# Splitting 1024-column weight tiles in one piece instead of two halves, in a two-layer transformer kernel on one Trainium2 core

## The chip, the cores and the metric

The kernel runs on one core of one Trainium2 chip. The metric is device time in microseconds for one call; smaller is better. The engines named here are PE (TensorE, matrix products; PEld is its weight load), ACT (ScalarE), DVE (VectorE), POOL (GpSimd) and SP (SyncE, which issues most DMAs). They run side by side, each through its own list of instructions in order, and meet at semaphores.

## What is computed

A trunk of two layers on 256 tokens of width 1024, in float32. Each layer has attention and then a product-key expert retrieval (PEER) over 16384 experts. The kernel does not gather the chosen experts; it multiplies by the whole tables and uses gates that are zero for the experts not chosen.

```python
q = xt @ w_q                                   # 8 heads, 2 x 128 wide
sc = q . sub_keys                              # 128 scores per head and side
v1,i1 = top_k(sc[:,:,0],16); v2,i2 = top_k(sc[:,:,1],16)
top_v, top_pos = top_k(all sums v1+v2, 16)     # expert index eidx = i1*128+i2
gates = softmax(top_v)
a = gelu(u_tab[eidx] @ x) * gates              # u_tab, v_tab: (16384, 1024)
out = sum_k a * v_tab[eidx]
```

## The kernel before

Each layer ends with `experts(l)`, and that part is most of the time. It has two passes, each over 128 tiles (`NKEY`) of 128 x 1024 float32, 512 KB each: the up pass (products with u, then GELU, spilled to DRAM as `s_store`), and the down pass (the spilled values come back, are weighted by the gates, and are multiplied with v). For accuracy each weight tile is split into `hi` (the value rounded to fp32r) and `lo` (the rest), and each product is made of three: hi with hi, hi with lo, lo with hi.

How one tile n travels:

- SP loads it into `raw`, a ring of four (`load_u`, `load_v`, lines 289 and 292), once the tile four before it has been lowered. In the up pass each load is followed by `spill` (L296), which stores the GELU result of eight tiles earlier. In the down pass each load follows a `fetch` (L302) of a spilled tile.
- ACT copies `raw` to `hi` (`split`, L742). `hi` and `lo` are rings of two, so tile n can be split only once PE has used tile n-2; this is counted by `w_used`. Before, a tile is two halves of 512 columns, each with its own split and its own wait on `w_used`.
- DVE writes `lo = raw - hi` (`lower`, L1061), again in two halves.
- PE runs `up` (24 matmuls of 256 columns, 12 per half) or `down` (12 matmuls of 512 columns, 6 per half). It waits for `hi_done` and `lo_done` ahead of each half, and raises `w_used` after each half.

What else stands in the queues, in program order:

- ACT in the up pass, step n: split half 0 of tile n+2, `gelu(n)` (L748; it waits for the spill of tile n-4 to land), split half 1 of tile n+2. In the down pass, step j: `split_a(j+1)` (L770, the hi part of the activations), then both halves of tile j+2.
- DVE in the down pass, step j: `weigh(j+2)` (L1075), `lower_a(j+1)` (L1080), then `lower` of tile j+2. In layer 0 every fourth step adds `next_modulation` (L1085 and L1088), a row of the next layer's modulation. PE's `down(j)` waits for `a_hi`, `a_lo`, `hi` and `lo` of tile j, in this order.
- DVE in the first 38 up tiles: the retrieval (top-16 searches, then `choose`). The heads 0 to 4 are done before; those of heads 5 to 7 (48 pieces) and `choose` (21 pieces) are a generator with an estimated cost per piece, 500 to 1200 ns. After each lowered half `advance(700)` takes pieces until their estimates reach 700; an overshoot is not carried over. `choose` has eight comparisons (L1045), each followed by a product on POOL (L400). It needs `q_e` from ACT (an Exp, L794), which stands between two loops of up steps.
- After tile 37 PE does `picks`; tiles 40 to 103 each have a group of matmuls, a `one_hot` on DVE and a `copy_gates` on ACT (L764); tiles 104 to 127 are plain up steps.

Of the kernel before, what the change touches and what calls it, by code (L numbers as in the profile page):

```python
# [15 lines left out]
P = 128  # L16
# [92 lines left out]
def build(nc, a, out):  # L109

    with ExitStack() as ctx:
# [155 lines left out]
        def _(sp):  # L267
# [19 lines left out]
            for l in range(LAYERS):  # L287
# [32 lines left out]
                for n in range(4, 8):  # L320
                    sp.wait_ge(s[l]["lo_done"], 2 * n - 6)
# [9 lines left out]
                for n in range(NKEY, NKEY + 8):  # L331
                    if n >= NKEY + 5:
                        fetch(n - NKEY - 1, (n - 1) % 4, 1)
                    sp.wait_ge(s[l]["lo_done"], 2 * n - 6)
# [3 lines left out]
                def down_loads(j, i, r):  # L338
                    fetch(j - 1, (r - 1) % 4, i - (1 if r == 0 else 0))
                    sp.wait_ge(s[l]["lo_done"], STREAM - 6 + 2 * j)  # L340
# [16 lines left out]
                sp.wait_ge(s[l]["lo_done"], 2 * STREAM)  # L357
# [46 lines left out]
        def _(pe):  # L404
# [148 lines left out]
            def experts(l):  # L553

                def up(n, r, wait=True):
# [23 lines left out]
                def down(j, r, first=False, end=False):  # L579

                    pe.wait_ge(s[l]["ah_done"], j + 1)
                    pe.wait_ge(s[l]["al_done"], j + 1)
                    for h in range(2):
                        pe.wait_ge(s[l]["hi_done"], STREAM + 2 * j + h + 1)
                        pe.wait_ge(s[l]["lo_done"], STREAM + 2 * j + h + 1)
# [6 lines left out]
                        last.then_inc(s[l]["w_used"], 1)  # L592
# [57 lines left out]
        def _(act):  # L650
# [67 lines left out]
            for l in range(LAYERS):  # L718
# [47 lines left out]
                def split_a(j, r, b, wait=True):  # L766
                    act.wait_ge(s[l]["a_ready"], j + 1)
                    if wait:
                        act.wait_ge(s[l]["w_used"], STREAM + 2 * j - 2)
# [6 lines left out]
                for h in range(PH):  # L776
# [8 lines left out]
                    if h in (4, 5):  # L785
                        for half in range(2):
                            split(h - 4, h - 4, half, 0, False)
# [19 lines left out]
                def down_step(j, r, round_, wait=True, more=True):  # L807
                    split_a(j + 1, r + 1, (r + 1) % 4, wait)
                    if more:
                        nr, nround = (r + 2) % 4, round_ + (r + 2) // 4 + NKEY // 4  # L810
                        for h in range(2):
                            split(NKEY + 2 + j, nr, h, nround)
# [8 lines left out]
                for n in range(0, 4, 2):  # L821
                    act.wait_ge(s[l]["w_used"], 2 * STREAM)
# [5 lines left out]
        def _(dve):  # L828
# [227 lines left out]
            def experts(l):  # L1056

                def lower(n, r, h):
                    dve.wait_ge(s[l]["hi_done"], 2 * n + h + 1)
                    c = slice(h * HALF, (h + 1) * HALF)  # L1060
                    v.tensor_tensor(lo[:, r % 2, c], raw[:, r, c], hi[:, r % 2, c].bitcast(F32), ALU.subtract).then_inc(s[l]["lo_done"], 1)  # L1061
# [39 lines left out]
                for h in range(PLAIN_HEADS):  # L1101
                    for _ in retrieve_head(l, h):
                        pass
                    if h == 3:
                        for n in range(2):
                            for half in range(2):
                                lower(n, n, half)
                for n in range(GROUP_AT - 2):
                    for half in range(2):
# [207 lines left out]
```

## Time and profile before

| what | value |
|---|---|
| median of 3 runs | 2355.55 us (2352.31 to 2356.49) |
| the profiled execution | 2345.75 us, its span 2343.8 us |
| PE busy | 2114.5 us (90%) |
| DVE busy | 1505.0 us (64%) |
| ACT busy | 1026.7 us (44%) |
| matmuls of the down pass, a_hi with hi | 1024 of 396 ns |
| lowered halves, splits | 1024 of 690 ns, 1024 of 629 ns |

Times in the trace are microseconds from the start of the span. A row of a timeline has: start, duration, engine, line, operation, output<-inputs, shape, count, and in brackets the idle time of the engine ahead of it and what ended it. Matmuls overlap in the engine, so the distance from one start to the next is the time that one costs; the end of a matmul is modelled.

### The profile page before, as it was taken

The numbers are of one execution on the slowest core, as the hardware profiler recorded it, in microseconds if no ns is written. First come the engines' busy times: TensorE is split into PE (matmuls) and PEld (weight loads), VectorE is DVE, ScalarE is ACT, GpSimd is POOL, SyncE is SP. The second block draws the span as 40 slices with busy tenths as digits, with TensorE's granted clock in tenths as the row PEclk, the third lists the DMA queues.
The fourth block names the chain that finished last, engine by engine and source line by source line (L and its number), as shares of the span: only waits on it lengthen the run. The fifth ranks groups of instructions, "written<-read, shape, count | busy, mean of one in ns | idle before, by whom it ended". The sixth has DMA issues, their size and how long they took to land.

```text
span 2343.8 us, 43649 instructions
## 1 busy us (share of the span) xinstructions
PE 2114.5 (90%) x12524; PEld 1860.3 (79%) x12524; DVE 1505.0 (64%) x3632; ACT 1026.7 (44%) x2019; POOL 62.9 (3%) x55
## 2 busy tenths in 40 slices
PE   1997699799999988888898889979999999999997
PEld 0844589799999976767676667979999998888886
DVE  5433778627777457777775226883677755777776
ACT  1013124535555445455453222345455554555554
POOL 0000000300000000000000000030000000000000
PEclk7976799899999999999999989989999999999999
DMA  7851426446555678788772213445455567777774
GB/s 262 337 214 72 135 90 190 145 123 174 173 175 172 205 243 287 275 296 295 284 255 77 90 72 108 144 144 170 135 171 176 172 197 231 238 240 237 239 240 150
DMA packets 168450, 447.24 MB, mean 191 GB/s; under 512 B 18624, under 2 KB 85440, under 8 KB 163792
## 3 DMA queue, kind: packets, MB, share of 16 engines
q1 hardware_dynamic: 163472, 393.17, 52.8%
q0 software_dynamic: 4928, 53.45, 5.7%
q8 instruction: 26, 0.43, 0.1%
q14 instruction: 24, 0.20, 0.0%
HBM read 409.84 MB, written 36.70 MB: 191 GB/s over the span
## 4 chain that ended last, share of the span: by engine, by line
PE 73%; DVE 12%; DMA 7%; ACT 4%; issue 3%; SPq 1%; ACTq 0%; DVEq 0%
PE bank L406 72%; DMA s_store<-work 3%; DVE lo L1061 3%; DMA wmod_ring<-s_store 2%; DVE big L1045 2%; ACT hi L742 2%; DMA wmod_ring<-in_w_mod 1%; DVE wmod_ring L1085 1%; ACT big L697 1%; ACT a_hi L770 1%; DVE wmod_ring L1075 1%; PE bank L461 1%; DVE big L906 0%; DVE work L848 0%; DVE big L997 0%
## 5 line engine op out<-in xcount | busy, mean ns | idle before, releaser
L1061 DVE TENSOR_TENSOR lo<-raw,hi 128x512 fp32r<-128x512 f32 x1024 | 697.3, 690 | 460.8 <-ACT hi L742 455.8
L742 ACT ACTIVATE hi<-raw 128x512 fp32r<-128x512 f32 x1024 | 634.7, 629 | 507.9 <-PE bank L406 505.5
L406 PE MATMUL bank<-x_hi,hi 128*128 128x256 f32 x2048 | 599.9, 293 | 39.6 <-DVE lo L1061 25.7
L406 PE MATMUL bank<-x_lo,hi 128*128 128x256 f32 x2048 | 582.5, 284 | 0.0
L406 PE MATMUL bank<-x_hi,lo 128*128 128x256 f32 x2048 | 582.0, 284 | 0.0
L406 PE MATMUL bank<-hi,a_hi 128*128 128x512 f32 x1024 | 405.1, 396 | 52.5 <-ACT a_hi L770 48.9
L406 PEld LDWEIGHTS bank<-x_hi,hi 128*128 128x128 f32 x2048 | 394.4, 193 | 52.3 <-issue 45.1
L406 PE MATMUL bank<-hi,a_lo 128*128 128x512 f32 x1024 | 402.1, 393 | 0.0
L406 PE MATMUL bank<-lo,a_hi 128*128 128x512 f32 x1024 | 401.5, 392 | 0.0
L406 PEld LDWEIGHTS bank<-x_lo,hi 128*128 128x128 f32 x2048 | 395.4, 193 | 0.2
L406 PEld LDWEIGHTS bank<-x_hi,lo 128*128 128x128 f32 x2048 | 394.9, 193 | 0.0
L406 PE MATMUL bank<-raw,big 128*128 128x256 f32 (+1 forms) x1248 | 285.0, 389 | 68.2 <-ACT raw L673 53.5
L406 PEld LDWEIGHTS bank<-raw,big 128*128 128x128 f32 (+1 forms) x1248 | 241.4, 195 | 107.2 <-issue 55.8
L406 PEld LDWEIGHTS bank<-hi,a_hi 128*128 128x128 f32 x1024 | 193.0, 188 | 115.0 <-ACT hi L742 54.5
L748 ACT ACTIVATE work<-bank 128x256 f32<-128x256 f32 x256 | 98.4, 384 | 308.1 <-DMA s_store<-work 190.7
L406 PEld LDWEIGHTS bank<-hi,a_lo 128*128 128x128 f32 x1024 | 193.3, 189 | 42.3
L406 PEld LDWEIGHTS bank<-lo,a_hi 128*128 128x128 f32 x1024 | 193.5, 189 | 35.5
L1069 DVE TENSOR_SCALAR wmod_ring<-cst,wmod_ring 128x128 f32<-128x128 f32 x512 | 142.2, 341 | 0.0
L406 PE MATMUL bank<-wmod_ring 128*128 128x128 f32 x1024 | 135.1, 275 | 0.0
L406 PEld LDWEIGHTS bank<-wmod_ring 128*128 128x128 f32 x1024 | 125.7, 192 | 0.0
L1075 DVE TENSOR_TENSOR wmod_ring<-wmod_ring,big 128x256 f32<-128x256 f32 x256 | 107.2, 419 | 13.5 <-DMA wmod_ring<-s_store 13.3
L1080 DVE TENSOR_TENSOR a_lo<-wmod_ring,a_hi 128x256 fp32r<-128x256 f32 x256 | 106.9, 417 | 0.0
(138 smaller groups left out, 1432.4 us busy)
## 6 DMA issues: line engine op xcount, KB each, us to landing
raw<-in_u SPq DMA_DIRECT2D x256, 512.0 KB, 3.8
raw<-in_v SPq DMA_DIRECT2D x256, 512.0 KB, 3.9
wmod_ring<-in_w_mod SPq DMA_DIRECT2D x96, 512.0 KB, 4.6
s_store<-work SPq DMA_DIRECT2D x256, 128.0 KB, 3.6
wmod_ring<-s_store SPq DMA_DIRECT2D x256, 128.0 KB, 3.5
big<-in_w_in POOLq DMA_DIRECT2D x10, 2048.0 KB, 11.1
big<-in_w_q POOLq DMA_DIRECT2D x16, 1024.0 KB, 6.2
big<-in_w_out POOLq DMA_DIRECT2D x2, 4096.0 KB, 12.8
```

The costliest lines, as they stand in the source:

```text
L406: return nc.tensor.matmul(o, w, x, start=start, stop=stop, skip_group_check=free)
L461: last = nc.tensor.transpose(bank[4 + n % 2][:, c * P:(c + 1) * P], scores[:, i, c * P:(c + 1) * P], ident)
L697: last = f(c, c, ACT.Exp, bias=neg[:, 2 * i + t:2 * i + t + 1], accum_out=den[:, 2 * i + t:2 * i + t + 1])
L742: f(hi[:, r % 2, c], raw[:, r, c], ACT.Copy).then_inc(s[l]["hi_done"], 1)
L748: f(work[:, r, :], bank[4 + r % 2][:, 0:T], ACT.Gelu).then_inc(s[l]["s_gelu"], 1)
L770: f(a_hi[:, r % 2, :], back[:, b, :], ACT.Copy).then_inc(s[l]["ah_done"], 1)
L1045: v.tensor_tensor(q_hot[n // 2].rearrange("p h k a -> p (h k) a")[:, c], q_abf[side][:, t, c].unsqueeze(2).to_broadcast([P, 64, TOPK]), io ...
L1061: v.tensor_tensor(lo[:, r % 2, c], raw[:, r, c], hi[:, r % 2, c].bitcast(F32), ALU.subtract).then_inc(s[l]["lo_done"], 1)
L1069: ins = v.tensor_scalar(hot[r % 2][:, 1, n, :], iota, pick[:, 1, bass.ds(4 * g + n, 1)], pick[:, 2, bass.ds(4 * g + n, 1)], ALU.is_equal, ...
L1075: v.tensor_tensor(back[:, b, :], back[:, b, :], gates[:, bass.ds(j, 1), :].rearrange("p a t -> p (a t)"), ALU.mult)\
L1080: v.tensor_tensor(a_lo[:, r % 2, :], back[:, b, :], a_hi[:, r % 2, :].bitcast(F32), ALU.subtract).then_inc(s[l]["al_done"], 1)
L1085: v.tensor_tensor_reduce(wmod_ring[:, r, :], wmod_ring[:, r, :], c_all[:], 1.0, 0.0, ALU.mult, ALU.add, tile_sum[:, r:r + 1]).then_inc(s[1 ...
```

## The change

Every weight tile is split and lowered whole: one `split` (ACT) and one `lower` (DVE) of 1024 columns, one pair of waits and one increment of `w_used` per tile on PE. All thresholds on `hi_done`, `lo_done` and `w_used` are counted in tiles. In an up step ACT does `split(n+2)` and then `gelu(n)`. `advance(700)` after each half becomes `advance(1400)` after each tile, and the Exp of the gates moves from behind up step 15 to behind up step 23. The diff is cut to its core; the other hunks change thresholds and loops in the same way.

```diff
@@ -318,11 +318,11 @@
                 with sp.Fori(2, NKEY // 4) as i:
                     for r in range(4):
-                        sp.wait_ge(s[l]["lo_done"], 8 * i + 2 * r - 6)
+                        sp.wait_ge(s[l]["lo_done"], 4 * i + r - 3)
                         load_u(4 * i + r, r)
                         spill(4 * i + r - 8, r)
                 sp.wait_ge(s[l]["hot_used"], GROUPS)
...
@@ -557,15 +557,14 @@
                     o = bank[4 + r][:, 0:T]
-                    for h in range(2):
-                        pe.wait_ge(s[l]["hi_done"], 2 * n + h + 1)
-                        pe.wait_ge(s[l]["lo_done"], 2 * n + h + 1)
-                        for k in range(h * KT // 2, (h + 1) * KT // 2):
-                            c = slice(k * P, (k + 1) * P)
-                            mm(o, hi[:, r, c], x_hi[:, k, :], k == 0, False)
-                            mm(o, hi[:, r, c], x_lo[:, k, :], False, False)
-                            last = mm(o, lo[:, r, c], x_hi[:, k, :], False, k == KT - 1)
-                        last.then_inc(s[l]["w_used"], 1)
+                    pe.wait_ge(s[l]["hi_done"], n + 1)
+                    pe.wait_ge(s[l]["lo_done"], n + 1)
+                    for k in range(KT):
+                        c = slice(k * P, (k + 1) * P)
+                        mm(o, hi[:, r, c], x_hi[:, k, :], k == 0, False)
+                        mm(o, hi[:, r, c], x_lo[:, k, :], False, False)
+                        last = mm(o, lo[:, r, c], x_hi[:, k, :], False, k == KT - 1)
+                    last.then_inc(s[l]["w_used"], 1)
...
@@ -580,16 +579,16 @@
                     pe.wait_ge(s[l]["al_done"], j + 1)
+                    pe.wait_ge(s[l]["hi_done"], NKEY + j + 1)
+                    pe.wait_ge(s[l]["lo_done"], NKEY + j + 1)
                     for h in range(2):
-                        pe.wait_ge(s[l]["hi_done"], STREAM + 2 * j + h + 1)
-                        pe.wait_ge(s[l]["lo_done"], STREAM + 2 * j + h + 1)
                         c = slice(h * HALF, (h + 1) * HALF)
                         for t in range(TT):
                             o, tok = bank[2 * t + h][:, :], slice(t * P, (t + 1) * P)
                             mm(o, a_hi[:, r, tok], hi[:, r, c], first, False, True)
                             mm(o, a_hi[:, r, tok], lo[:, r, c], False, False, True)
                             last = mm(o, a_lo[:, r, tok], hi[:, r, c], False, end, True)
-                        last.then_inc(s[l]["w_used"], 1)
+                    last.then_inc(s[l]["w_used"], 1)
...
@@ -734,24 +733,22 @@
-                def split(n, r, h, round_, wait=True):
+                def split(n, r, round_, wait=True):
                     act.wait_ge(raw_in[r], 16 * (round_ + 1) + 16 * l * (STREAM // RAWS))
                     if wait:
-                        act.wait_ge(s[l]["w_used"], 2 * n + h - 3)
-                    c = slice(h * HALF, (h + 1) * HALF)
-                    f(hi[:, r % 2, c], raw[:, r, c], ACT.Copy).then_inc(s[l]["hi_done"], 1)
+                        act.wait_ge(s[l]["w_used"], n - 1)
+                    f(hi[:, r % 2, :], raw[:, r, :], ACT.Copy).then_inc(s[l]["hi_done"], 1)
 
                 def gelu(n, r, round_, wait=True):
-                    act.wait_ge(s[l]["w_used"], 2 * n + 2)
+                    act.wait_ge(s[l]["w_used"], n + 1)
                     if wait:
                         act.wait_ge(s_out[r], 16 * round_ + 16 * l * (NKEY // STAGES))
                     f(work[:, r, :], bank[4 + r % 2][:, 0:T], ACT.Gelu).then_inc(s[l]["s_gelu"], 1)
 
                 def up_step(n, r, round_, wait=True):
                     nr, nround = (r + 2) % 4, round_ + (r + 2) // 4
-                    split(n + 2, nr, 0, nround)
+                    split(n + 2, nr, nround)
                     gelu(n, r, round_, wait)
-                    split(n + 2, nr, 1, nround)
 
...
@@ -783,16 +780,15 @@
-                up_steps(4, 16)
+                up_steps(4, 24)
                 act.wait_ge(s[l]["gate_max"], 1)
                 f(q_e[:], q_e[:], ACT.Exp).then_inc(s[l]["gate_exp"], 1)
-                up_steps(16, GROUP_AT)
+                up_steps(24, GROUP_AT)
...
@@ -1055,10 +1050,9 @@
-                def lower(n, r, h):
-                    dve.wait_ge(s[l]["hi_done"], 2 * n + h + 1)
-                    c = slice(h * HALF, (h + 1) * HALF)
-                    v.tensor_tensor(lo[:, r % 2, c], raw[:, r, c], hi[:, r % 2, c].bitcast(F32), ALU.subtract).then_inc(s[l]["lo_done"], 1)
+                def lower(n, r):
+                    dve.wait_ge(s[l]["hi_done"], n + 1)
+                    v.tensor_tensor(lo[:, r % 2, :], raw[:, r, :], hi[:, r % 2, :].bitcast(F32), ALU.subtract).then_inc(s[l]["lo_done"], 1)
...
@@ -1103,12 +1097,10 @@
                 for n in range(GROUP_AT - 2):
-                    for half in range(2):
-                        lower(n + 2, (n + 2) % 4, half)
-                        advance(700)
+                    lower(n + 2, (n + 2) % 4)
+                    advance(1400)
...
                 def down_step(j, r, round_, mods=None, weighs=True, lowers=True):
                     if weighs:
                         weigh(j + 2, (r + 2) % 4, round_ + (r + 2) // 4)
                     lower_a(j + 1, r + 1, (r + 1) % 4)
                     if lowers:
-                        for half in range(2):
-                            lower(NKEY + 2 + j, (r + 2) % 4, half)
+                        lower(NKEY + 2 + j, (r + 2) % 4)
```

## Rows read from the trace of the kernel before

**Rows 1.** The chain that ended last, shares of the span by engine.

```profile
PE 73%; DVE 12%; DMA 7%; ACT 4%; issue 3%; SPq 1%; ACTq 0%; DVEq 0%
```

**Rows 2.** Stages: start:end, length, busy of PE, PEld, DVE, ACT, POOL; clock, DMA, GB/s.

```profile
356.57:439.36 82.79, 67.89 (x495) 63.72 (x494) 78.29 (x213) 36.87 (x68) 22.06 (x8) 0.92 0.54 164
771.00:844.50 73.50, 70.51 (x577) 69.51 (x576) 32.19 (x51) 34.80 (x73) 0.00 (x0) 1.00 0.72 214
844.50:1256.40 411.90, 362.67 (x1536) 286.67 (x1536) 298.95 (x606) 202.54 (x382) 3.76 (x7) 0.99 0.77 272
1971.40:2325.00 353.60, 353.27 (x1536) 288.47 (x1536) 260.49 (x508) 199.56 (x382) 0.00 (x0) 1.00 0.73 234
```

**Rows 3.** Groups by line and shape: count, busy us, mean ns, idle before.

```profile
L1208 DVE TENSOR_TENSOR x_lo<-raw,x_hi 128x2048 fp32r<-128x2048 f32 x2 | 4.6, 2294 | 5.1 <-ACT x_hi L735 5.1
L735 ACT ACTIVATE x_hi<-raw 128x2048 fp32r<-128x2048 f32 x2 | 3.8, 1910 | 0.1
```

**Rows 4.** Timeline of the down pass, layer 1, at the end of a tile.

```profile
2102.18 0.40 PE L406 MATMUL bank<-hi,a_hi 128*128 128x512 f32 x1
...
2102.38 0.63 ACT L742 ACTIVATE hi<-raw 128x512 fp32r<-128x512 f32 x1 [0.75 <-PE bank L406]
2102.41 0.40 PE L406 MATMUL bank<-lo,a_hi 128*128 128x512 f32 x1
...
2103.05 0.69 DVE L1061 TENSOR_TENSOR lo<-raw,hi 128x512 fp32r<-128x512 f32 x1 [0.69 <-ACT hi L742]
...
2103.66 0.42 DVE L1075 TENSOR_TENSOR wmod_ring<-wmod_ring,big 128x256 f32<-128x256 f32 x1
...
2103.99 0.42 DVE L1080 TENSOR_TENSOR a_lo<-wmod_ring,a_hi 128x256 fp32r<-128x256 f32 x1
```

**Rows 5.** Timeline of the down pass, layer 0, from one modulation step to the next.

```profile
1015.02 0.47 PE L406 MATMUL bank<-hi,a_hi 128*128 128x512 f32 x1 [1.23 <-ACT a_hi L770]
...
1018.06 0.63 ACT L742 ACTIVATE hi<-raw 128x512 fp32r<-128x512 f32 x1 [0.75 <-PE bank L406]
...
1023.51 0.63 ACT L742 ACTIVATE hi<-raw 128x512 fp32r<-128x512 f32 x1 [0.73 <-PE bank L406]
...
1024.78 1.22 DVE L1085 CUSTOM_DVE_ANT_0 wmod_ring<-wmod_ring,c_all 128x1024 f32<-128x1024 f32 x1
...
1026.65 0.42 DVE L1080 TENSOR_TENSOR a_lo<-wmod_ring,a_hi 128x256 fp32r<-128x256 f32 x1
...
1027.42 0.47 PE L406 MATMUL bank<-hi,a_hi 128*128 128x512 f32 x1 [1.21 <-ACT a_hi L770]
```

**Rows 6.** Timeline of DVE, POOL and PE in the first up tiles, layer 0.

```profile
359.23 0.69 DVE L1061 TENSOR_TENSOR lo<-raw,hi 128x512 fp32r<-128x512 f32 x1 [5.02 <-ACT hi L742]
...
400.23 0.42 DVE L1019 TENSOR_TENSOR big<-big 128x256 f32<-128x256 f32 x1
...
438.54 2.48 DVE L1061 TENSOR_TENSOR lo<-raw,hi 128x512 fp32r<-128x512 f32 x4
...
408.13 2.75 POOL L400 TENSOR_TENSOR big<-big 128x1024 f32<-128x1024 f32 x1 [83.47 <-DVE big L1045]
...
408.56 3.40 DVE L1045 TENSOR_TENSOR big<-big,cst 128x1024 f32<-128x1024 f32 x1
...
411.89 0.68 DVE L1061 TENSOR_TENSOR lo<-raw,hi 128x512 fp32r<-128x512 f32 x1
...
412.71 0.43 PE L406 MATMUL bank<-x_hi,hi 128*128 128x256 f32 x1 [2.26 <-DVE lo L1061]
```

**Rows 7.** Timeline of ACT and PE where a loop of up steps begins anew, layer 0.

```profile
466.62 1.28 ACT L742 ACT_TABLE_LOAD   x1
...
470.48 0.36 PE L406 MATMUL bank<-x_hi,hi 128*128 128x256 f32 x1 [1.05 <-ACT work L748]
```

**Rows 8.** Timeline of DVE and ACT in the last up tiles, layer 0.

```profile
820.60 1.29 DVE L1061 TENSOR_TENSOR lo<-raw,hi 128x512 fp32r<-128x512 f32 x2 [1.83 <-ACT hi L742]
...
825.70 0.38 ACT L748 ACTIVATE work<-bank 128x256 f32<-128x256 f32 x1 [1.75 <-DMA s_store<-work]
```

More of the change, by code:

```diff
@@ L320, in _ @@
                 for n in range(4, 8):
-                    sp.wait_ge(s[l]["lo_done"], 2 * n - 6)
+                    sp.wait_ge(s[l]["lo_done"], n - 3)
                     load_u(n, n % 4)
@@ L333, in _ @@
                         fetch(n - NKEY - 1, (n - 1) % 4, 1)
-                    sp.wait_ge(s[l]["lo_done"], 2 * n - 6)
+                    sp.wait_ge(s[l]["lo_done"], n - 3)
                     load_v(n - NKEY, n % 4)
@@ L339, in down_loads @@
                     fetch(j - 1, (r - 1) % 4, i - (1 if r == 0 else 0))
-                    sp.wait_ge(s[l]["lo_done"], STREAM - 6 + 2 * j)
+                    sp.wait_ge(s[l]["lo_done"], NKEY - 3 + j)
                     load_v(j, r)
@@ L356, in _ @@
                 fetch(NKEY - 1, 3, NKEY // 4 - 1)
-                sp.wait_ge(s[l]["lo_done"], 2 * STREAM)
+                sp.wait_ge(s[l]["lo_done"], STREAM)
                 sp.dma_start(raw[:, 0:2].rearrange("p a n -> p (a n)"), x_store).then_inc(x_back, 16)
@@ L768, in split_a @@
                     if wait:
-                        act.wait_ge(s[l]["w_used"], STREAM + 2 * j - 2)
+                        act.wait_ge(s[l]["w_used"], NKEY + j - 1)
                     f(a_hi[:, r % 2, :], back[:, b, :], ACT.Copy).then_inc(s[l]["ah_done"], 1)
@@ L785, in _ @@
                     if h in (4, 5):
-                        for half in range(2):
-                            split(h - 4, h - 4, half, 0, False)
+                        split(h - 4, h - 4, 0, False)
                 copy_keys(PH - 1)
@@ L810, in down_step @@
                         nr, nround = (r + 2) % 4, round_ + (r + 2) // 4 + NKEY // 4
-                        for h in range(2):
-                            split(NKEY + 2 + j, nr, h, nround)
+                        split(NKEY + 2 + j, nr, nround)
                 for r in range(4):
@@ L821, in _ @@
                 for n in range(0, 4, 2):
-                    act.wait_ge(s[l]["w_used"], 2 * STREAM)
+                    act.wait_ge(s[l]["w_used"], STREAM)
                     f(yt[:, n // 2, 0:512], bank[n][:, :], ACT.Copy).then_inc(s[l]["e_copied"], 1)
@@ L1105, in experts @@
                         for n in range(2):
-                            for half in range(2):
-                                lower(n, n, half)
+                            lower(n, n)
                 for n in range(GROUP_AT - 2):
-                    for half in range(2):
-                        lower(n + 2, (n + 2) % 4, half)
-                        advance(700)
+                    lower(n + 2, (n + 2) % 4)
+                    advance(1400)
                 for _ in left:
@@ L1118, in experts @@
                 for g in range(4):
-                    for half in range(2):
-                        lower(GROUP_AT + g, g, half)
+                    lower(GROUP_AT + g, g)
                     one_hot(g, g, g >= 2)
@@ L1123, in experts @@
                     for r in range(4):
-                        for half in range(2):
-                            lower(GROUP_AT + 4 * i + r, r, half)
+                        lower(GROUP_AT + 4 * i + r, r)
                         one_hot(4 * i + r, r)
@@ L1128, in experts @@
                     for r in range(4):
-                        for half in range(2):
-                            lower(4 * i + r, r, half)
+                        lower(4 * i + r, r)
                 dve.wait_ge(s[l]["g_copied"], GROUPS)
@@ L1135, in experts @@
                         lower_a(0, 0, 0)
-                    for half in range(2):
-                        lower(NKEY + n, n, half)
+                    lower(NKEY + n, n)
                 def down_step(j, r, round_, mods=None, weighs=True, lowers=True):
@@ L1143, in down_step @@
                     if lowers:
-                        for half in range(2):
-                            lower(NKEY + 2 + j, (r + 2) % 4, half)
+                        lower(NKEY + 2 + j, (r + 2) % 4)
                     if mods:
@@ L1213, in _ @@
                 for n in range(1, 4, 2):
-                    dve.wait_ge(s[l]["w_used"], 2 * STREAM)
+                    dve.wait_ge(s[l]["w_used"], STREAM)
                     v.tensor_copy(yt[:, n // 2, 512:1024], bank[n][:, :]).then_inc(s[l]["e_copied"], 1)
```

## The prediction, made before the changed kernel was run

> **What bounds the kernel now.** I read the chain that ended last first: PE has 73% of it [rows 1], so what counts is whether PE waits. The second view is the table of stages [rows 2]. In the down pass of layer 1 PE is busy 353.27 of 353.60 us: 128 tiles at 2.76 us, PE alone is the bound. In the down pass of layer 0 it is busy 362.67 of 411.90 us, in the last 24 up tiles 70.51 of 73.50, and in the first 20 or so up tiles 67.89 of 82.79. The third view is the timeline of one tile in each of these, to see how late hi and lo come. A tile n can only be split when tile n-2 has been used. So each tile closes a loop with the one two before it: S(j+2) = S(j) + one tile of PE + the chain ACT, DVE, PE. PE hides this chain as long as the loop is shorter than two PE tiles. That is what the change touches.
>
> **The down pass, the loop before.** Sizes, start to start: split of the last half to its lower 0.67 (2102.38 to 2103.05), lower to weigh 0.61 (to 2103.66), weigh to lower_a 0.33 [rows 4]; lower_a itself 0.42, and from its end to PE's first matmul 0.35 (1026.65 + 0.42 = 1027.07, to 1027.42) [rows 5]. Together 2.38. From a tile's first matmul to the split that its end releases: 1018.06 - 1015.02 = 3.04 where PE had stood still before it [rows 5]; the 12 matmuls step by 0.23, so that is 2.76 + 0.08 for the start from rest + 0.20 of hand-over; without rest 2.95. Loop: 2.95 + 2.38 = 5.33, against 2 x 2.76 = 5.52. PE hides it with 0.19 to spare, as layer 1 shows. The same sum tells the modulation step of layer 0: 1023.51 to 1027.42 = 3.91, which is 2.38 + 1.53 for L1085 and L1088, and four tiles take 1027.42 - 1015.02 = 12.40, not 11.04 [rows 5].
>
> **The loop after.** The last half is no longer all that is left when a tile ends; the whole tile is. A split of 1024 columns: 630 ns at 512 [rows 4] and 1910 at 2048 [rows 3] give 0.834 ns a column and 1056 ns, 0.43 more than a half. A lower: 690 at 512 (0.69 in the rows) [rows 4] and 2294 at 2048 [rows 3] give 1.04 ns a column and 1225 ns, 0.535 more. The loop grows by 0.96 to 6.29 us, and PE, which now rests once a loop, adds its 0.08: 6.37 for two tiles, 3.19 a tile (one of the two tiles waits, the other starts right behind it). Layer 1: 128 x (3.19 - 2.76) = +55 us. Layer 0, four tiles: the loop with the modulation is 6.37 + 1.53 = 7.90, the other 6.37, together 14.27 against 12.40; 32 times 1.87 = +60 us. Layer 0 also has waits that are not of this loop: 411.90 - 32 x 12.40 = 15 us, mostly late fetches beside POOL's large loads. A fetch is asked for three tiles ahead, which are now 1.4 us longer; I let half of it (8 us, bounds 0 and 15) disappear: +52. The two waits and one increment fewer on PE cost nothing now: across the middle of two tiles' halves the matmuls step by 0.23 (2102.18 to 2102.41) as everywhere [rows 4], so nothing is gained.
>
> The Trainium skill, TensorE: Matmul & The Clock Gate, "The cost: per-tile semaphore tail", says that increments of packed matmuls serialize at some 26 ns each. For 512 increments fewer that would be an estimate of 13 us gained; the rows above show no such step here.
>
> **The up pass, plain tiles.** The 24 matmuls step by 0.12: 2.88 a tile. The loop is 2.88 + 0.20 + 1.10 (split to lower) + 1.225 + 0.14 (lower's end to PE: 411.89 + 0.68 is 412.57, PE starts at 412.71 [rows 6]) = 5.55, below 5.76: hidden by 0.2. `gelu` now stands behind the split. That removes a stall: before, the second half's split stood behind `gelu`, and `gelu` behind the spill's landing (lowered 821.3, gelu 825.70 [rows 8]), a loop of about 6.0 for two tiles. After, gelu(n) is due at S(n) + 4.1 and must be done by S(n) + 5.8, and the next split is due only then. The last 24 tiles go from 73.5 us [rows 2] to 24 x 2.88 = 69.1 and a little at the change of pass: -4 a layer. The 64 group tiles take 3.76 each (group and up), so the loop has nearly 2 us to spare: nothing.
>
> **The first 40 up tiles.** Here DVE sets the pace: the pieces of the retrieval stand between the lowers. Before, 359.23 to 400.23 for 12 tiles (4 pieces a tile: the estimates are 500 and 550, so two pass each 700) is 3.4 us a tile; then `choose` to 438.54 [rows 6], with 12 halves of 0.60 in it, so 31.1 us of its own. There each L1045 takes 3.32 instead of 1.2 because a POOL product (2.75) runs first [rows 6]. After, three pieces a tile: 1.66 (41.0 less 24 x 0.60, over 48 pieces, x 3) + 1.145 = 2.81, below PE's 2.88. The 48 pieces last 16 tiles at PE's pace, and `choose` takes 7 tiles: 31.1 + 7 x 1.145 = 39.1. Reckoned from tile 0 at 356.57 [rows 2]: lower(18) at 356.57 + 16 x 2.88 + 4.2 = 406.8, lower(25) at 445.9, PE in tile 25 at 447.3, thirteen tiles later `picks` at 484.7. Before, PE was in the middle of tile 20 at 439.36, 17.5 tiles ahead of `picks` (489.8), and lost 1.05 on three restarts of the ACT loop, where two table loads of 1.28 stand ahead of the split and the gelu [rows 7], and some more beside them; by its matmuls `picks` began at about 495.8. After, the first of these loads runs ahead of the wait and the second behind the split; bank and ring bear 0.2. Gain 11; I take 9, because PE now rests 4.8 us at a stretch in `choose`, and the clock, 0.92 in this stage [rows 2], may be longer at its lower level; -9 a layer, bounds 0 and -16 (two L1045 side by side might leave POOL out). The Exp moved behind step 23 is early enough: step 23 ends some 3.5 us before lower(24), and `choose` asks for it after that. No queue is moved otherwise; SP's loads and spills wait for the same tiles, lowered at most 0.5 us later, with over 5 us to spare.
>
> The Trainium skill, VectorE: DVE Perf Modes, "The TRN2 errata", says that an instruction with its source in SBUF pays a fixed latency, and that larger tiles spread it; that speaks for the change. The rows agree: two lowered halves take 1.29 [rows 8], a whole one 1.225. It pays only where DVE is the bound.
>
> **Sum.** +55 + 52 - 2 x 4 - 2 x 9 = +81. On the profiled execution (span 2343.8, 2345.75 us in all) that is 2427; the median of the runs shown is 2355.55, 0.4% above that execution, and a difference carries over: 2355.55 + 81 = 2437.
>
> **Rivals.** (A) The loop stays hidden. It decides at a chain of 2 x 2.76 - 2.95 = 2.57 from split to PE; I have 3.34. If weigh and lower_a (0.75) turned out not to lie on it, for instance because DVE does them while the whole split runs, the down pass costs nothing and the gains remain: 2355.55 - 26 = 2330, faster. Against: in program order they stand behind `lower` of the tile, and the 12.40 of layer 0 comes out only with them. Chance 0.04. (B) A shorter loop: the 0.20 of hand-over and the 0.08 are not paid by a warm pipeline: 0.14 less a tile, 256 tiles, 36 us less: 2401. Against: 3.04 is measured. Chance 0.12. (C) The gains don't come (9 a layer lost to the slower clock and to POOL in the way of the longer lowers) and the 8 us of late fetches stay: 2355.55 + 81 + 26 = 2463. Chance 0.14. (D) The middle of a tile costs PE something after all: at most 0.01 a boundary by [rows 4], 512 boundaries, 5 us: 2432. Chance 0.02.
>
> **Chances and range.** The forecast has 0.68, its own range being +-14 by the bounds above. The range from B to nearly C, 2403 to 2460, leaves out A and part of B and C, some 0.2. A measurement of this kernel tells about 0.2% (5 us) from no change; faster 0.04 (A), within 0.01, slower 0.95.
>
> **What would show it.** In layer 1's down pass: one wait of PE in two tiles, each about 0.8 us, ended by lower_a; two tiles in 6.37; the stage 408 us instead of 353.6. In layer 0: four tiles in 14.27, the stage about 464. In the plain up tiles 2.88 a tile and no gelu waiting on PE's path; `picks` of layer 0 some 10 us earlier; no 1.05 waits behind table loads. A hi of 1056 and a lo of 1225 ns. Wrong would be: stages of the down pass under 390 us (then A or B), or up tiles with waits for lo (then the up loop, with only 0.2 us to spare, is the part that I mis-sized).

## The result, and the profile after

| | before | after |
|---|---|---|
| median of 4 runs each | 2354.98 us (2352.31 to 2356.49) | 2448.33 us (2444.6 to 2452.5) |
| ratio after / before | | 1.0398, 95% interval 1.0378 to 1.0418 |
| span of the profiled execution | 2343.8 us | 2444.8 us |
| PE busy | 2114.5 us (90%) | 2153.6 us (88%) |

The change makes the kernel slower by 93 us, where +81 was forecast. The chain by engine, from the page of after (compare [rows 1]):

```profile
PE 73%; DVE 11%; ACT 6%; issue 6%; DMA 4%; SPq 0%; DVEq 0%; ACTq 0%
```

The shares hardly move: PE has 73% as before, and DVE and ACT have 17% between them instead of 16%, of a span that is 101 us longer (some 416 us against 375). The chain alone does not say where the time went; the stages below do. The three groups of the page that matter (line, engine, operation, output<-inputs, count | busy us, mean ns of one | idle before them, what ended most of it):

```profile
L1055 DVE TENSOR_TENSOR lo<-raw,hi 128x1024 fp32r<-128x1024 f32 x512 | 639.6, 1250 | 613.1 <-ACT hi L740 611.3
L740 ACT ACTIVATE hi<-raw 128x1024 fp32r<-128x1024 f32 x512 | 542.1, 1059 | 975.5 <-PE bank L406 974.4
L406 PE MATMUL bank<-hi,a_hi 128*128 128x512 f32 x1024 | 423.3, 413 | 117.3 <-ACT a_hi L767 66.2
```

A split takes 1059 ns (forecast 1056). A lower takes 1250 on average, because of some in the retrieval that take far longer; in the down pass it is 1230 (forecast 1225). The 117.3 us in the last row are PE's rests ahead of the down tiles of both layers. The table of stages, as in [rows 2]; it is of the first 20 or so up tiles, the down pass of layer 0 and that of layer 1:

```profile
360.64:445.38 84.74, 74.24 (x580) 73.24 (x578) 76.36 (x194) 36.88 (x51) 20.95 (x7) 0.94 0.63 191
838.44:1315.44 477.00, 387.05 (x1537) 294.14 (x1537) 284.31 (x481) 177.80 (x257) 3.77 (x7) 0.96 0.68 235
2019.13:2427.05 407.92, 378.61 (x1537) 278.44 (x1537) 241.76 (x382) 174.58 (x257) 0.00 (x0) 1.00 0.65 203
```

The down pass of layer 1 takes 407.9 us instead of 354.7 to the same end ([rows 2] stop 1 us earlier, at 353.6), with PE at the same full clock and busy 378.6. The timeline of two of its tiles, DVE, ACT and each tile's first matmul:

```profile
2025.24 1.06 ACT L740 ACTIVATE hi<-raw 128x1024 fp32r<-128x1024 f32 x1 [1.68 <-PE bank L406]
2025.53 0.47 PE L406 MATMUL bank<-hi,a_hi 128*128 128x512 f32 x1 [0.38 <-DVE a_lo L1074]
...
2026.33 1.23 DVE L1055 TENSOR_TENSOR lo<-raw,hi 128x1024 fp32r<-128x1024 f32 x1 [1.15 <-ACT hi L740]
...
2028.58 0.47 PE L406 MATMUL bank<-hi,a_hi 128*128 128x512 f32 x1
2028.63 1.06 ACT L740 ACTIVATE hi<-raw 128x1024 fp32r<-128x1024 f32 x1 [2.02 <-PE bank L406]
...
2029.72 1.23 DVE L1055 TENSOR_TENSOR lo<-raw,hi 128x1024 fp32r<-128x1024 f32 x1 [1.50 <-ACT hi L740]
...
2030.86 0.42 DVE L1069 TENSOR_TENSOR wmod_ring<-wmod_ring,big 128x256 f32<-128x256 f32 x1
2031.20 0.42 DVE L1074 TENSOR_TENSOR a_lo<-wmod_ring,a_hi 128x256 fp32r<-128x256 f32 x1
2031.96 0.47 PE L406 MATMUL bank<-hi,a_hi 128*128 128x512 f32 x1 [0.39 <-DVE a_lo L1074]
```

Follow one turn of the loop: the tile from 2025.53 ends and releases the split at 2028.63; lower 2029.72, weigh 2030.86, lower_a 2031.20, and PE starts at 2031.96, 6.43 after 2025.53. PE runs two tiles per turn and then stands until lower_a is done.

Where the time went, from the profiled executions, each stage from its first matmul to that of the next (us). "Retrieval" is the up pass to the first group of matmuls, "rest of up" from there to the down pass:

| stage | before | after | difference | forecast |
|---|---|---|---|---|
| ahead of the experts (code unchanged) | 356.6 | 360.6 | +4.0 | 0 |
| retrieval, layer 0 / 1 | 176.1 / 175.7 | 169.1 / 169.3 | -7.0 / -6.4 | -9 / -9 |
| rest of up, layer 0 / 1 | 311.8 / 311.7 | 308.7 / 308.5 | -3.1 / -3.2 | -4 / -4 |
| down pass, layer 0 | 413.2 | 477.0 | +63.8 | +52 |
| down pass, layer 1 | 354.7 | 407.9 | +53.2 | +55 |

Without the first row that is +97, sixteen above the sum of the prediction, and most of it is in one stage, the down pass of layer 0. The start of the program varies between 356 and 362 us over all kernels here, none of which changes it.

### The profile page after: what moved, and what is told of

Same layout as the page of the kernel before. It is cut to its first block, busy times and chain, and to the rows that moved or that the text cites. A ratio compares the mean times of both kernels' runs of the same rounds, so it can differ in the third digit from the quotient of the medians.

```text
span 2444.8 us, 40461 instructions
## 1 busy us (share of the span) xinstructions
PE 2153.6 (88%) x12524; PEld 1857.0 (76%) x12524; DVE 1450.0 (59%) x3120; ACT 918.9 (38%) x1499; POOL 69.6 (3%) x55
## 4 chain that ended last, share of the span: by engine, by line
PE 73%; DVE 11%; ACT 6%; issue 6%; DMA 4%; SPq 0%; DVEq 0%; ACTq 0%
PE bank L406 72%; ACT hi L740 4%; DMA wmod_ring<-in_w_mod 2%; DVE lo L1055 2%; DVE big L1040 1%; DVE wmod_ring L1069 1%; DVE wmod_ring L1079 1%; DMA wmod_ring<-s_store 1%; DVE a_lo L1074 1%; ACT big L696 1%; DMA s_store<-work 1%; PE bank L461 0%; ACT a_hi L767 0%; DVE big L901 0%; DVE work L843 0%
## 5 line engine op out<-in xcount | busy, mean ns | idle before, releaser
L1055 DVE TENSOR_TENSOR lo<-raw,hi 128x1024 fp32r<-128x1024 f32 x512 | 639.6, 1250 | 613.1 <-ACT hi L740 611.3
L740 ACT ACTIVATE hi<-raw 128x1024 fp32r<-128x1024 f32 x512 | 542.1, 1059 | 975.5 <-PE bank L406 974.4
L406 PE MATMUL bank<-hi,a_hi 128*128 128x512 f32 x1024 | 423.3, 413 | 117.3 <-ACT a_hi L767 66.2
L406 PE MATMUL bank<-hi,a_lo 128*128 128x512 f32 x1024 | 407.1, 398 | 0.0
L406 PE MATMUL bank<-lo,a_hi 128*128 128x512 f32 x1024 | 406.6, 397 | 0.0
L767 ACT ACTIVATE a_hi<-wmod_ring 128x256 fp32r<-128x256 f32 x256 | 103.0, 402 | 16.1 <-DVE wmod_ring L1069 16.0
```

The costliest lines, as they stand in the source:

```text
L406: return nc.tensor.matmul(o, w, x, start=start, stop=stop, skip_group_check=free)
L740: f(hi[:, r % 2, :], raw[:, r, :], ACT.Copy).then_inc(s[l]["hi_done"], 1)
L767: f(a_hi[:, r % 2, :], back[:, b, :], ACT.Copy).then_inc(s[l]["ah_done"], 1)
L1055: v.tensor_tensor(lo[:, r % 2, :], raw[:, r, :], hi[:, r % 2, :].bitcast(F32), ALU.subtract).then_inc(s[l]["lo_done"], 1)
```

## The experiments

In all of them the number of pieces per tile can be chosen for each pass and each engine, and the thresholds follow it. The edits are shown shortened, by the names of the steps and without their arguments. Each difference is against the median of before that was run beside it (2351.47 to 2352.92 us).

### Is it the down pass alone, and do the parts add up?

`e1_up_whole` has whole tiles in the up pass (with the new order of `gelu`, `advance(1400)` and the later Exp) and halves in the down pass; `e2_down_whole` the other way round.

```diff
 # pieces per tile: split, lower, increments of w_used
-up   2, 2, 2    down 2, 2, 2
+up   1, 1, 1    down 2, 2, 2      (e1_up_whole)
+up   2, 2, 2    down 1, 1, 1      (e2_down_whole)
```

> Up pass as in the changed kernel (whole tiles, gelu behind the split, three retrieval pieces a tile, Exp behind step 23), down pass in halves as before. Theory (the loop over two ring slots in the down pass is what costs): only the gains remain, 7 us in the first 40 tiles and 3 us in the rest of the up pass, in each layer; 2355 - 20 = 2335 us, down stages 413 and 355 us as before. Rival (whole instructions cost wherever they stand, by longer waits of PE for lo or by burstier loads): slower than 2355.

> Down pass whole, up pass in halves as before. Theory: down stages 477 and 408 us as in the changed kernel, no gains: 2355 + 64 + 53 = 2472 us. Rival (the two passes share a cause, such as the order of the loads): the two parts don't add up to the +93 of the whole change, off by over 15 us.

Measured: e1_up_whole 2325.15 us, ratio 0.9891 (0.9873 to 0.9908); e2_down_whole 2468.99, ratio 1.0497 (1.0475 to 1.0519). That is -28 and about +116; their sum is +88, and the whole change +93, so the two passes are nearly independent. The gain of the up pass is close to the -26 of the prediction; this run was put at 2335. The down pass of e2_down_whole, layer 0 and layer 1:

```profile
850.08:1326.01 475.93, 386.84 (x1537) 293.49 (x1537) 284.36 (x481) 177.71 (x257) 3.76 (x7) 0.96 0.67 236
2039.42:2447.80 408.38, 377.86 (x1537) 278.34 (x1537) 241.80 (x382) 174.48 (x257) 0.00 (x0) 1.00 0.63 203
```

Both are within 1.1 us of the stages of after: what the down pass loses does not hang on the up pass.

### Which of the two instructions makes the loop long?

`e3_split_halves` is the change with the split and `w_used` of the down pass in halves again, the lower still whole. `e4_lower_halves` has only the lower in halves, the split whole.

```diff
-down 1, 1, 1
+down 2, 1, 2      (e3_split_halves)
+down 1, 2, 1      (e4_lower_halves)
```

> Changed kernel, but in the down pass ACT splits in halves again, each released by PE's half; DVE still lowers the whole tile. Theory: the loop loses 0.43 us (one half's split instead of the whole): 5.94 for two tiles, layer 1's down pass 381 us instead of 408, layer 0's 4 tiles 13.4, some 440 us; in all 2384 us. Rival (the long lower alone holds PE): no change, 2448 us.

> Changed kernel, but in the down pass DVE lowers in halves again and PE waits for each half's lo; ACT splits whole. Theory: weigh and lower_a stand behind both halves in DVE's order and PE asks for a_lo first, so nothing is gained: the loop grows by 0.07, 2448 + 5 = 2453 us, layer 1's down pass 412 us. Rival (PE waits for the long lower and could start on half a tile): the loop loses 0.6 us, 38 us a layer, 2371 us.

Measured: e3_split_halves 2386.05, ratio 1.0135 (1.0112 to 1.0158); e4_lower_halves 2457.75, ratio 1.0444 (1.042 to 1.0469). Their down passes of layer 1, first e3_split_halves:

```profile
1982.79:2367.84 385.05, 368.90 (x1537) 282.19 (x1537) 241.76 (x382) 200.51 (x384) 0.00 (x0) 1.00 0.67 215
```

and e4_lower_halves:

```profile
2030.47:2444.37 413.90, 377.70 (x1537) 279.56 (x1537) 250.54 (x509) 174.51 (x257) 0.00 (x0) 1.00 0.62 200
```

Halved splits take 385.05 / 64 = 6.02 us for two tiles, 0.36 less than after: the first half is copied while PE still works on the second (the loop gives back nearly the 0.43 of the prediction). Halved lowers behind a whole split take 413.90 / 64 = 6.47, 0.10 more: neither half can start before the whole split is done, and two pieces take longer than one. So it isn't the size of the lower by itself: a halved split pays with the lower whole, a halved lower behind a whole split does not. The rival that put the loop down to the lower, at 2371, fell. The layer 0 stage gives more than the loop: 442.4 against 477.0, where 64 times 0.36 is 23; the next experiment shows why.

### Is the order on DVE on the loop?

In the prediction weigh and lower_a stand behind the lower on the loop (rival A said they do not). In `e5_weigh_first` a step first lowers the activations of tile j+1 and only then weighs those of tile j+3, so that of the two only lower_a stands between a tile's lower and PE.

```diff
 def down_step(...):
-    weigh(j + 2, ...)
     lower_a(j + 1, ...)
+    weigh(j + 3, (r + 3) % 4, round_ + (r + 3) // 4)
     lower(j + 2, ...)
```

> Changed kernel with one order on DVE changed in the down pass: step j does lower_a(j+1), weigh(j+3), lower(j+2), so that weigh no longer stands between the lower of a tile and its lower_a. Theory (a loop over two tiles that runs through ACT, DVE and PE in their program order): weigh's 0.33 us leaves the loop, 6.04 for two tiles, layer 1's down pass 387 us instead of 408, layer 0 some 456 instead of 477; in all 2448 - 42 = 2406 us. Rival (PE waits for hi and lo of the tile only, not for what follows on DVE): no change, 2448 us.

Measured: 2390.89 us, ratio 1.0159 (1.014 to 1.0178), fifteen below what was expected. The first matmul of a turn in layer 1, and its down passes:

```profile
2018.11 0.47 PE L412 MATMUL bank<-hi,a_hi 128*128 128x512 f32 x1 [0.36 <-DVE a_lo L1120]
...
2024.19 0.47 PE L412 MATMUL bank<-hi,a_hi 128*128 128x512 f32 x1 [0.35 <-DVE a_lo L1120]
```

```profile
834.82:1280.74 445.92, 371.90 (x1537) 284.70 (x1537) 281.32 (x481) 174.45 (x257) 3.76 (x7) 0.99 0.73 252
1984.57:2374.98 390.41, 367.61 (x1536) 282.43 (x1536) 241.72 (x382) 174.56 (x257) 0.00 (x0) 1.00 0.67 212
```

Two tiles take 6.08 us, as expected; 64 x 6.08 = 389 and the stage is 390.4. In layer 0 64 x 0.29 = 19 us would be due, but the stage is 31 shorter (477.0 to 445.9), and its clock is 0.99 instead of 0.96. Here is what stands behind it in the trace of after. PE's matmuls at one modulation tile of layer 0:

```profile
989.15 0.47 PE L406 MATMUL bank<-hi,a_hi 128*128 128x512 f32 x1 [2.15 <-ACT a_hi L767]
...
989.68 0.54 PE L406 MATMUL bank<-hi,a_lo 128*128 128x512 f32 x1
990.02 0.63 PE L406 MATMUL bank<-hi,a_hi 128*128 128x512 f32 x1
990.45 0.63 PE L406 MATMUL bank<-lo,a_hi 128*128 128x512 f32 x1
...
992.58 0.63 PE L406 MATMUL bank<-hi,a_hi 128*128 128x512 f32 x1
993.01 0.48 PE L406 MATMUL bank<-lo,a_hi 128*128 128x512 f32 x1
993.33 0.39 PE L406 MATMUL bank<-hi,a_lo 128*128 128x512 f32 x1
...
997.08 0.47 PE L406 MATMUL bank<-hi,a_hi 128*128 128x512 f32 x1 [0.65 <-DVE a_lo L1074]
```

From 990.02 to 993.01 they start 0.43 apart instead of 0.23. The clock of that stretch, and of one ten us later (columns as in [rows 2]):

```profile
989.70:992.70 3.00, 3.00 (x9) 2.33 (x8) 0.91 (x3) 0.00 (x0) 0.00 (x0) 0.51 0.63 194
1000.30:1003.70 3.40, 2.49 (x11) 1.71 (x10) 2.37 (x3) 2.05 (x3) 0.00 (x0) 1.00 0.70 253
```

The granted clock is 0.51: TensorE runs at the lower of its two levels, 1.2 instead of 2.4 GHz. It had just rested 2.15 us, behind the modulation work on DVE. ACT's next split, released by this tile's end, comes at 993.75 instead of 992.2, and the following turn starts 7.93 after this one instead of 6.37. Such a stretch has seven or eight starts of 0.43 as a rule, some 1.5 us (two long ones, in e3_split_halves and e5_weigh_first, have twelve and thirteen). In the down pass of layer 0 the trace of before has 2 of them, after 11, e5_weigh_first 2, e3_split_halves 2. Each stands right behind a rest of PE. In that stage of after PE has 28 rests over 1.8 us, and 11 of them were followed by such a stretch. In e5_weigh_first the same rest behind the modulation is 1.7 us long (29 of them), and none was; its two stretches follow rests of 5.0 and 3.7 us. Two more rests behind the modulation in after, and two in e5_weigh_first, each pair four tiles apart:

```profile
1004.98 0.47 PE L406 MATMUL bank<-hi,a_hi 128*128 128x512 f32 x1 [2.19 <-ACT a_hi L767]
1019.23 0.47 PE L406 MATMUL bank<-hi,a_hi 128*128 128x512 f32 x1 [2.19 <-ACT a_hi L767]
```

```profile
990.84 0.47 PE L412 MATMUL bank<-hi,a_hi 128*128 128x512 f32 x1 [1.73 <-ACT a_hi L800]
1004.30 0.47 PE L412 MATMUL bank<-hi,a_hi 128*128 128x512 f32 x1 [1.76 <-DVE a_lo L1120]
```

In after four tiles take 14.25 us without a stretch (1004.98 to 1019.23) and 15.83 with one (989.15 to 1004.98). Nine of its eleven stretches stand behind a modulation step; those nine groups of four tiles are 1.2 to 1.6 us longer than 14.27, 12.7 us in all. The two of before follow other rests, of 4.4 and 3.4 us. So 9 stretches more than before, some 13 us, belong to layer 0 of the change. e2_down_whole, with the same down pass, has 10 stretches in a stage of the same length (475.9).

The loop itself gives more in layer 0 than in layer 1: four tiles of e5_weigh_first take 13.46 (990.84 to 1004.30), 0.79 less, or 25 us for 32 times. With the 13 of the clock that is 38, where 31 was measured. In e3_split_halves they take 13.44 (1198.94 to 1212.38), 26 us for 32 times, and 26 + 13 = 39, where 34.6 was measured. The 7 and 4 us that go the other way are not resolved, and why the loop gives 0.79 and not twice 0.29 was not tested.

### Does the modulation's place matter?

`e6_mod_first` has the change and moves the modulation ahead of the lower of tile j+2, where DVE waits for the split anyway; weigh and lower_a stay ahead of it as in the change.

```diff
     ...
+    if mods:
+        next_modulation(*mods)
     lower(j + 2, ...)
-    if mods:
-        next_modulation(*mods)
```

> Changed kernel with the modulation of layer 0's down pass ahead of lower(j+2) instead of behind it. DVE waits there for the split anyway. Theory: the 1.53 us leaves the loop; four tiles 12.74 instead of 14.27, PE's rests stay at about 0.7 us, and the dips of the clock that the rests of 2.2 us bring (11 stretches of 3.4 us at half speed in layer 0's down pass) go with them: 408 + 5 instead of 477 us, in all 2384 us; layer 1 stays at 408. Rival (the clock falls here for another reason, such as POOL's large loads or the length of the pass): the dips remain, 15 us more, 2399 us.

Measured: 2399.36, ratio 1.0198 (1.018 to 1.0215). Expected was 2384, with the rival at 2399. The four tiles do take 12.72 us, as expected (the turns of PE start at 918.53, 924.91, 931.25), but the stage is 438.6 us, not 413. Two rows of what is left, and the waits of DVE for the fetched values (total us, times, longest), between 880 and 1250:

```profile
950.41 0.47 PE L412 MATMUL bank<-hi,a_hi 128*128 128x512 f32 x1 [0.29 <-DVE a_lo L1120]
954.14 0.42 DVE L1115 TENSOR_TENSOR wmod_ring<-wmod_ring,big 128x256 f32<-128x256 f32 x1 [1.67 <-DMA wmod_ring<-s_store]
955.25 0.47 PE L412 MATMUL bank<-hi,a_hi 128*128 128x512 f32 x1 [1.88 <-ACT a_hi L800]
```

```profile
DVE wmod_ring L1115 <- DMA wmod_ring<-s_store: 12.3, 5, 4.4
```

A fetch lands late, PE rests 1.88 us, and again a stretch at half speed follows (the matmuls from 956.35 on). The trace has 6 such places, none behind DVE's own modulation work: five at late fetches, where PE rests 13.0 us in all, and one ahead of the window of these waits, at the start of the pass:

```profile
855.74 0.77 PE L412 MATMUL bank<-hi,a_hi 128*128 128x512 f32 x1 [7.37 <-ACT a_hi L800]
```

There DVE had waited 6.97 us for the load of the modulation's row (before and after have the same rest, 4.4 and 5.0 us long). 32 x 12.72 = 407, the late fetches 13, this rest 7 and the slow stretches some 10 (51 starts that are 0.20 longer) make 437 of the 438.6. The number of the rival was met, but neither side had the reason whole: the modulation left the loop, as the theory has it, and late loads came in its place.

### Both moves together

`e9_both_first` has whole tiles, weigh early and the modulation ahead of the lower.

> Changed kernel with both orders of DVE's down pass changed: lower_a(j+1), weigh(j+3), the modulation, lower(j+2). Theory: the loop stays at 6.08 us as in e5, above PE's 5.52, and the modulation costs 0.2 a time: layer 1's down pass 390 us, layer 0's 393 + 25 for late fetches and their clock dips = 418; in all 2391 - 28 = 2363 us, still not below the kernel before: with two slots and a whole tile on the loop PE can't be fed. Rival (with both out of the way PE is fed): layer 1's down pass near 355, 2310 us.

Measured: 2369.28, ratio 1.0075 (1.0051 to 1.0099), six above what was expected, with down passes of 425.5 and 387.1 us. The rival, at 2310, fell. Even with both orders changed, whole tiles in the down pass stay 17 us behind before: two tiles take 387.1 / 64 = 6.05 us, over PE's 5.52.

### What gives the gain of the up pass?

Three things changed there. `e7_gelu_last` is the kernel before, with halves, and only `gelu` behind the second half's split; `e8_advance_late` is the kernel before with only the retrieval's pieces taken per tile, and the Exp later.

```diff
 # e7_gelu_last, up_step
     split(n + 2, half 0)
-    gelu(n)
     split(n + 2, half 1)
+    gelu(n)
 # e8_advance_late
     lower(n + 2, half 0)
-    advance(700)
     lower(n + 2, half 1)
-    advance(700)
+    advance(1400)
```

> Kernel before with one order changed on ACT in the up pass: both halves of the split, then gelu. Nothing is whole. Theory (the gains of the up pass come in good part from gelu leaving the split's way): 3 us gained in the last 88 up tiles of each layer, and some 4 in the first 40 where the loop restarts with table loads: 2353 - 14 = 2339 us. Rival (the gain comes from whole tiles): no change, 2353.

> Kernel before with the retrieval pieces dealt out as in the changed kernel: none after the first lowered half, 1400 after the second, so three pieces a tile instead of four, and the Exp behind step 23. Nothing is whole. Theory: some 4 us gained in the first 40 tiles of each layer, 2353 - 8 = 2345; e7 and e8 together make most of the 28 us that the whole up pass gained. Rival (whole tiles on DVE make that gain): no change, 2353.

Measured: e7_gelu_last 2330.68, ratio 0.9905 (0.9888 to 0.9922); e8_advance_late 2345.64, ratio 0.9973 (0.9962 to 0.9985). That is -21 (7 us more than was expected) and -6, together -27, and e1_up_whole with whole tiles on top is -28. So, if the two add up, the whole tiles themselves give the up pass nothing that can be measured (the next pair of runs compares them directly); the gain is from the two changes of order that came with them. By stage: `gelu` last shortens the retrieval by 5.5 and 5.3 us and the rest of up by 4.3 and 4.1; `advance(1400)` only the retrieval, by 4.0 and 4.2.

### A version that beats both

If only the orders matter, halves with all the orders should be best. `e10_up_whole_down_halves` has the up pass of the change, and in the down pass halves, weigh early and the modulation ahead of the lower; `e11_halves_everywhere` has halves in the up pass too, with `gelu` last and `advance(1400)`.

```diff
+up   1, 1, 1    down 2, 2, 2      (e10_up_whole_down_halves)
+up   2, 2, 2    down 2, 2, 2      (e11_halves_everywhere)
-    weigh(j + 2, ...)
     lower_a(j + 1, ...)
+    weigh(j + 3, ...)
+    if mods:
+        next_modulation(*mods)
     lower(j + 2, ...)
-    if mods:
-        next_modulation(*mods)
```

> Whole tiles in the up pass (e1), halves in the down pass, there with both orders of e9 on DVE. Theory: the loop in halves is 5.33 - 0.33 = 5.00, hidden; the modulation leaves it and costs some 0.2 of its 1.36 a time: layer 0's down pass 32 x 11.3 + 20 = 381 instead of 415, layer 1's 353 as before; 2325 - 34 = 2291 us. Rival (DVE is the bound of these steps): no gain in layer 0, 2325.

> No whole tile at all: the kernel before with gelu behind both halves of the split (e7), the retrieval pieces behind the second half (e8), and both orders of e9 in the down pass. Theory (the gains of the changed kernel are those of its order, not of its size): the same as e10 within 4 us, 2291. Rival (whole tiles give the up pass something of their own): e10 is faster by over 5 us.

Measured: e10_up_whole_down_halves 2309.39, ratio 0.9833 (0.981 to 0.9856); e11_halves_everywhere 2301.67, ratio 0.9795 (0.9769 to 0.982), the fastest version here, 50 us less than the runs of before beside it. Of the 8 us between the two 5 lie in the unchanged start, and their intervals overlap. The up passes of e11_halves_everywhere, from the first matmul to the down pass, take 473.6 and 472.0 us, those of e10_up_whole_down_halves 475.1 and 475.5: the rival, that whole tiles give the up pass something of their own, fell. Both versions were expected at 2291. Layer 1 is where it was expected (353; it takes 350), layer 0 is not (381; it takes 400 and 404); the down passes of e11_halves_everywhere, and its waits for fetches and for lower_a between 840 and 1230:

```profile
829.76:1233.62 403.86, 372.71 (x1537) 295.68 (x1537) 296.31 (x608) 200.89 (x384) 3.77 (x7) 0.95 0.80 278
1931.68:2281.81 350.13, 348.73 (x1536) 288.10 (x1536) 261.51 (x509) 200.91 (x384) 0.00 (x0) 1.00 0.76 237
```

```profile
DVE wmod_ring L1115 <- DMA wmod_ring<-s_store: 35.6, 18, 7.6
PE bank L412 <- DVE a_lo L1120: 28.4, 7, 6.5
```

The worst one in the timeline:

```profile
1139.61 0.43 DVE L1115 TENSOR_TENSOR wmod_ring<-wmod_ring,big 128x256 f32<-128x256 f32 x1 [7.57 <-DMA wmod_ring<-s_store]
...
1141.93 0.77 PE L412 MATMUL bank<-hi,a_hi 128*128 128x512 f32 x1 [6.53 <-DVE a_lo L1120]
```

With the loop off the path, the stage of 404 us has loads that land late as its largest loss (28 us of PE's rests in seven places; the stage has 6 slow stretches). One rest, of 5.8 us at the start of the pass, waits for the modulation's row. Five, of 2.8 to 6.5 us, are late fetches, and each ends 12 to 18 us after POOL issued one of its large loads of the next layer's weights; that these loads are the cause is argued from the place alone. Whether moving those loads would bring layer 0 to the 350 us of layer 1 was not tried.

## Why the prediction was right, and where it was not

**The loop.** The chain from split to PE and PE's two tiles a turn were the right picture. Layer 1: 407.9 us against the 408 written down, +53.2 against +55. The turn shown is 6.43, but the next three are 6.37, 6.34 and 6.36, and the stage over 64 is 6.37, as written down. e3_split_halves, e4_lower_halves and e5_weigh_first change one link each and the stage follows (6.02, 6.47, 6.08).

**Layer 0, the term that was mis-sized.** +52 was +63.8. Four tiles were to take 14.27 us, and without a slow stretch they do (14.25 in the rows above). That gives 456.6; the stage is 477.0. Of the 20 left over, 11 slow stretches of 1.5 us are 16, so that some 4 are late loads, where before had 413.2 less 396.8 = 16, 3 of them in 2 such stretches. The relief of the late loads, put at -8 with bounds 0 and -15, comes by this subtraction to about -9; the rest at the start of the pass, which waits for the modulation's row and not for a fetch, is no part of it (4.4 us before, 5.0 after). What was missing is the clock: the prediction had PE rest behind each modulation step, longer than before by 0.96, and charged 0.08 for the start from rest. So +60 less 8 lacked a term of some 13 us, 9 stretches more. It looked at the clock only in `choose`. [Rows 5] show the rest of before at its shorter length with matmuls at full pace behind it, and nothing in the trace of before told what one of 2.2 us would do. But that trace has its two slow stretches in this very stage, behind rests of 4.4 and 3.4 us, and the prediction did not look at them.

**The retrieval.** -9 a layer was -7.0 and -6.4, inside the bounds (0, -16). The forecast laid the gain to fewer pieces per tile and to table loads out of the way; the 1.05 us waits behind them [rows 7] are gone (0.16 to 0.24 remain). e7_gelu_last shows that more than half of the gain is `gelu` behind both splits. e1_up_whole, with the same up pass, has -8.9 and -8.7, and the eight profiled kernels with this up pass take 166.9 to 169.3 us for it, so the miss may be scatter between executions; what the long lowers in `choose` (below) take of it was not measured by itself.

**The plain up tiles.** -4 a layer was -3.1 and -3.2, and the reason is confirmed by e7_gelu_last, which gains 4.3 and 4.1 there with halves. The up loop, said to hide with 0.2 us to spare, does hide.

**PE's waits.** Dropping one pair of waits and one increment per tile gives nothing that these runs show: e7_gelu_last and e8_advance_late keep them all and together reach the gain of e1_up_whole within 1 us, and e11_halves_everywhere keeps them in an up pass that is 1.5 and 3.5 us shorter than that of e10_up_whole_down_halves. These comparisons cover the up pass, half of the increments. The estimate of 13 us by the Trainium skill (TensorE: Matmul & The Clock Gate, "The cost: per-tile semaphore tail") isn't borne out for these matmuls, as the rows had it. Nor does the saving of a fixed latency per instruction (the Trainium skill, VectorE: DVE Perf Modes, "The TRN2 errata") show in the time: DVE is busy 55 us less (1505.0 to 1450.0), and the up pass is no faster for it than with halves in the same order.

**The rivals.** A (the loop stays hidden, 2330) fell: weigh and lower_a are on the loop, and taking one of them off it shortens the loop by 0.29 (e5_weigh_first). B (a shorter loop, 2401) fell with the 6.37. C (2463) had its gains absent and its late fetches in place; both are refuted by the stages, although 2463 is not far from 2448. D (the middle of a tile costs PE something) fell: the matmuls still step by 0.23 from the first to the second half of a whole tile.

**The carry-over.** The sum was made on an execution of 2345.75 us and carried to the median. The spans of the two profiled executions differ by 101, 4 of it in the start, and the medians by 93: a difference of two single executions is good to some 8 us here, and the sum of 81 is to be read against that too.

## What to carry to other kernels

Where a ring has two slots, the piece size is not only an overhead: it is how much of the next tile's work can overlap the tile that still holds the slot. Write the loop out (slot released, chain over all engines, slot used, one tile of PE) before making pieces larger; here the spare was 0.19 us in 5.52 and the larger piece cost 0.96. And when a change bundles sizes with orders, measure them apart: here the orders were the gain, and the sizes the loss.

## What the runs showed of the hardware that was not expected

**A lower behind a POOL product.** In `choose` a comparison on DVE is followed by a product on POOL. The timeline of after:

```profile
420.78 1.22 DVE L1055 TENSOR_TENSOR lo<-raw,hi 128x1024 fp32r<-128x1024 f32 x1
420.95 3.30 POOL L400 TENSOR_TENSOR big<-big 128x1024 f32<-128x1024 f32 x1 [92.23 <-DVE big L1040]
...
425.41 6.57 POOL L400 TENSOR_TENSOR big<-big 128x1024 f32<-128x1024 f32 x2 [1.16 <-DVE big L1040]
426.39 3.36 DVE L1055 TENSOR_TENSOR lo<-raw,hi 128x1024 fp32r<-128x1024 f32 x1
...
429.89 0.45 PE L406 MATMUL bank<-x_hi,hi 128*128 128x256 f32 x1 [4.64 <-DVE lo L1055]
```

The lower takes 1.22 us where it starts ahead of the POOL product, and then the product is the longer one: it ends 2.25 us after the lower, 3.30 after its own start. Where the product was there first, the lower takes 3.36 and ends 1.09 after the first of the two products (at 428.66), and PE has waited 4.64 us. In before it was the comparison (L1045) that started behind the product and took 3.40 (the product 2.75), while the halved lower started ahead of it and kept its 0.68 [rows 6]. Both instructions have two inputs in SBUF, and in these rows they do not share the time: the second one stands until the first is through. The Trainium skill (GPSIMD Engine Reference, "1. Specifications") says that POOL's interfaces to SBUF are shared with VectorE, with contention for instructions that have two SBUF inputs; the trace agrees, and here the price is nearly the whole of the other instruction.

**Half clock behind rests of two microseconds.** The 2.15 us rest in the rows above was followed by matmuls 0.43 apart, in a stage where PE is busy 387.05 of 477.00 us. Of 28 rests over 1.8 us in that stage 11 had a slow stretch behind them, of 29 rests of 1.7 us in e5_weigh_first none; but in e6_mod_first one of 1.88 had. So the traces give no length at which it begins, and 17 of the 28 rests had no slow stretch behind them. Where it happens, the rest costs 1.2 to 1.6 us on top of its own 2.15.

**A spare that the busy share hid.** The down pass of layer 1 was read as bound by PE alone, 353.27 of 353.60 us [rows 2]. With lower_a ahead of weigh it takes 350.13 (e11_halves_everywhere), 2.735 us a tile instead of 2.76. What PE lost of it, 0.03 us a tile, shows in no wait of the trace of before; its cause stays open.
